# Rotary rows stored in reading order, values of four tiles kept in SBUF, and index queries loaded ahead of stores in an attention and DeltaNet layer

## The chip, the cores and the metric

The kernel runs on one core of a Trainium2 chip. The metric is the device time of one execution in microseconds; the time before is the median of three runs. Two kernels of this size can be told from each other when they differ by more than about 0.2%.

## The reference

One transformer-like layer over 2048 tokens with a model width of 1024, all in float32. In short:

```python
h = rms_norm(x, norm_mix_g)
qa, ka, va, qi, ki, wi, qb, kb, vb, zb, bb, ab = split(h @ w_in)
qa, ka, qi, ki = rope(qa), rope(ka), rope(qi), rope(ki)      # heads of 64
score[t, s] = sum_h wi[t, h] * relu(qi[t, h] . ki[s])        # 8 index heads
sel = top_k(score where s < limit(t), 256)                   # keys of each query
o_a = softmax(qa . ka[sel] / 8) @ va[sel]                    # 8 heads, 2 key heads
o_b = gated_deltanet(qb, kb, vb, zb, bb, ab)                 # 4 heads of 128
x = x + concat(o_a, o_b) @ w_out
x = x + square(relu(rms_norm(x, norm_ffn_g) @ w_ff1)) @ w_ff2
return rms_norm(x, norm_final_g)
```

Rotary embedding (rope) pairs feature i of a head with feature i + 32: each half of a head is multiplied by a cosine and added to the other half multiplied by a sine.

## The kernel before

Everything is kept transposed, features on partitions and tokens along the free dimension. The 2048 tokens are 16 tiles of 128. Three stages run one after the other, each a block in which every engine has its own queue of instructions, executed strictly in order; engines meet only at semaphores.

**Stage 1** (`norm_and_projection`) normalises x and projects the columns that the DeltaNet and the index need, into the DRAM tensor `projT`, one chunk of 128 features at a time.

**Stage 2** (`deltanet_and_selection`) runs the DeltaNet over the 16 tiles as 18 rounds of 22 slots (`ROUND`, L313). Into the same slots two planners put other work. `ProjectionPlan` (L329) puts the rest of the projection, 36 chains of 512 tokens by 128 features: index queries, attention queries (chunks 5 to 8), attention keys (chunk 9), values (chunk 10). A chain is two halves on TensorE, an eviction on ScalarE into the buffer `p_out` (`project_out`, L1104, waits until the store before it has landed) and a store by SyncE (SP) two slots later (`project_store`, L686). `SelectionPlan` (L379) puts the index scores and the search for the 256th largest score: `rotation` (L470) puts the load of a tile's index queries on SP (six transfers by `rotated_rows`, L492, and two of the rotary table), and from four slots later four steps on GpSimd (POOL), the multiply by cosine, the multiply by sine, the sum and the low part. Scores of that tile are put after the last of these, and the vector engine's share is spread over the slots by estimated costs. A load waits for the low part of the tile before, since `rot` is one buffer. In a slot, SP does the parts of the selection in the order in which they were put, and then those of the projection.

**Stage 3** (`attention_and_mlp`) overlaps attention with the output projection and the MLP. `OverlapPlan` (L1327) puts every step into numbered slots; within a slot the order of each engine is the list `ORDER` (L1335). Attention works in units, 4 for each tile (two heads each): scores against the keys, mask and exponential, transposes of the probabilities, their split into a high and a low part (`m_phi`, `m_plo`), and a product with the values. The first 16 units (tiles 0 to 3) run three slots apart, alone, before the dense matmuls begin at slot 0; this stretch is called the prelude below. From there on the dense matmuls fill TensorE and the units run beside them.

Each tile has three items to prepare (`prep_items`, L1374): its keys and two groups of four query heads. An item is loaded by SP (`prep_in`, L1639: six transfers, three for each half of the partitions), multiplied by cosine on DVE (`by_cosine`, L2012) and by sine on POOL (`by_sine`, L1738), added on POOL (`add`), rounded on ScalarE, and its low part taken on POOL (queries) or DVE (keys). Items 0 to 11 take turns in five buffers (four are rows of `m_acc`, the fifth is `m_rot`); from item 12 on all use `m_rot`, so that each load waits for the item before. The rotary table has one buffer, loaded by `table_load` (L1647), which waits until all three items of the tile before have been multiplied.

The values of a tile are loaded (`values_in`), transposed on TensorE, split into a high and a low part in the one buffer `v_split` (L1562), stored to the DRAM tensor `valsT` (`values_out`, L1659) and loaded again for each product, in pieces of at most two tiles (`values_back`, L1663), into four buffers `vals`. The load of the newest piece waits for the store:

```python
if m >= 4:
    sp.wait_ge(pv_done, m - 3)
if end == t + 1:
    sp.wait_ge(v_kept, 16 * (t + 1))
```

Weights of the dense matmuls are loaded by `weights` (L1634), rounded on ScalarE (L1848) and their low part taken on POOL (L1727); SP issues the third load only once the first of these low parts is there. In POOL's order a slot's weight split comes before the rotary steps.

Of the kernel before, what the change touches and what calls it, by code (L numbers as in the profile page):

```python
# [17 lines left out]
ALU = mybir.AluOpType  # L18
# [360 lines left out]
class SelectionPlan:  # L379
# [121 lines left out]
def deltanet_and_selection(nc, S, topk, projT, consts, mixT, biasT, scoreT, xhT, xlT, w_proj, shared, z_stored):  # L501
# [14 lines left out]
    with ExitStack() as ctx:  # L516
# [5 lines left out]
        p_out = sb("p_out", [P, 512])  # L522
# [61 lines left out]
        p_high, p_low, p_done, p_left, p_stored = map(sem, " p_high p_low p_done p_left p_stored".split())  # L584
# [51 lines left out]
        def _(sp):  # L636
# [15 lines left out]
            def selection(t, m):  # L652
                if t == 0 and m - 1 in KEY_STAGE and KEY_STAGE[m - 1] + 1 < S // KP:
                    load_keys(KEY_STAGE[m - 1] + 1)
                for kind, j in plan.at("sp", t, m):
                    if kind == "load":
# [5 lines left out]
                        if stored_chains:  # L662
                            sp.wait_ge(p_stored, 16 * (max(stored_chains) + 1))
# [64 lines left out]
            sp.wait_ge(p_stored, 16 * len(rest.chains))  # L728
# [242 lines left out]
        def _(act):  # L971
# [132 lines left out]
            def project_out(n):  # L1104
                act.wait_ge(p_done, 2 * (n + 1))
                if n:
                    act.wait_ge(p_stored, 16 * n)
                else:
                    for u in range(2):
                        act.wait_ge(z_stored[u], 16 * ((N_PROJECTED + 1 - u) // 2))  # L1110
                nc.scalar.activation(p_out[:, :], pps[:, :], ACT.Copy).then_inc(p_left, 1)
# [215 lines left out]
class OverlapPlan:  # L1327
# [72 lines left out]
    def attention(self):  # L1400
# [23 lines left out]
        for u in range(self.UN):  # L1424
# [12 lines left out]
            for i in range(self.turns(t)):  # L1437
# [9 lines left out]
                ready = kept[t] if i == self.turns(t) - 1 else self.first  # L1447
                self.put("sp", max(ready + 1, product_slot[m - 4] + 1 if m >= 4 else self.first), "values_back", u, i)
# [100 lines left out]
def attention_and_mlp(nc, S, topk, projT, consts, biasT, scoreT, valsT, mixT, xT, w_units, g_ffn, g_final, outT):  # L1549
# [5 lines left out]
    with ExitStack() as ctx:  # L1555
# [6 lines left out]
        v_split = sb("m_vsplit", [P, KV_HEADS, 2 * HD], f32r)  # L1562
# [60 lines left out]

        def prep_rows(i, half):
            r = acc[:, 2 * prep_slot(i):2 * prep_slot(i) + 2, :] if prep_slot(i) < 4 else rot[:, :, :]
            return r[:, half, 0:heads_of(i) * P].rearrange("p (h s) -> p h s", s=P)

        last_turn = lambda u: plan.turn[u, plan.turns(u // 4) - 1]
# [4 lines left out]
        def _(sp):  # L1633
# [25 lines left out]
            def values_out(t):  # L1659
                sp.wait_ge(v_done, t + 1)  # L1660
                sp.dma_start(valsT[t], v_split[:, :, :].rearrange("p g d -> p (g d)").bitcast(fp32)).then_inc(v_kept, 16)

            def values_back(u, i):  # L1663
                m, g, t = plan.turn[u, i], u % 4 // 2, u // 4
                end = min(2 * i + 2, t + 1)
                if m >= 4:
                    sp.wait_ge(pv_done, m - 3)
                if end == t + 1:
                    sp.wait_ge(v_kept, 16 * (t + 1))
                sp.dma_start(vals[:, m % 4, 0:end - 2 * i, :].bitcast(fp32),  # L1670
                             valsT[2 * i:end, :, g * P:(g + 1) * P].rearrange("c p d -> p c d")).then_inc(v_back[m % 4], 16)
# [48 lines left out]
        def _(pool):  # L1720
# [17 lines left out]
            def by_sine(i):  # L1738
                t = plan.prep_items[i][0]
                pool.wait_ge(rot_in[prep_slot(i)], 96 * (prep_turn(i) + 1))  # L1740
# [34 lines left out]
        def _(act):  # L1775
# [74 lines left out]
            def values_hi(t):  # L1850
                r = plan.ring_at["values", t]
                act.wait_ge(ring_done, r + 1)
                if t:
                    act.wait_ge(v_kept, 16 * t)
                nc.scalar.activation(v_split[:, :, 0:HD], t_bank(r)[:, 0:P].rearrange("p (g d) -> p g d", d=HD),
# [41 lines left out]
        def _(dve):  # L1897
# [95 lines left out]
            def values_low(t):  # L1993
                r = plan.ring_at["values", t]
                dve.wait_ge(v_high, t + 1)
                nc.vector.tensor_tensor(v_split[:, :, HD:2 * HD], t_bank(r)[:, 0:P].rearrange("p (g d) -> p g d", d=HD),
# [293 lines left out]
```

## Time and profile before

| | us |
|---|---|
| median of three runs | 3779.7 (3775.54 to 3780.05) |
| the profiled execution | 3773.35 |
| its span | 3771.5 |
| TensorE busy | 3343.0 (89% of the span) |
| ScalarE busy | 2162.8 (57%) |
| VectorE (DVE) busy | 2114.7 (56%) |
| GpSimd (POOL) busy | 1376.8 (37%) |

Stage 1 ends at about 489 us, stage 2 at about 1461 us and the prelude of stage 3 at about 1608 us of the span. A timeline row gives the start, the duration, the engine and line, the operation with output and inputs, and in brackets the idle time of the engine before it with what ended it. SPq rows are transfers issued by SyncE: the duration is that of the issue.

### The profile page before, as it was taken

To read this page: it belongs to the slowest core of one execution; us is meant where nothing else is said; L and a number is where in the kernel's file an instruction comes from. 1 tells how busy PE (TensorE), PEld (TensorE's weight loads), DVE (VectorE), ACT (ScalarE), POOL (GpSimd) and SP (SyncE) were. 2 spreads that over 40 slices of the span, in tenths; PEclk is the share of its full clock that TensorE was granted. 3 is DMA by queue.
4 is the path that set the end of the run, shared out by engine and by line. 5 is a ranking of instruction groups with operands and counts; after the bars stand their busy time and mean duration, and the time that the engine had idled before them with its cause. 6 is when DMAs were issued, how large, how long until landed. Compare 5 with 4: busy or idle time off the path is not lost.

```text
span 3771.5 us, 47140 instructions
## 1 busy us (share of the span) xinstructions
PE 3343.0 (89%) x16770; PEld 2754.8 (73%) x16770; DVE 2114.7 (56%) x3680; ACT 2162.8 (57%) x3717; POOL 1376.8 (37%) x721
## 2 busy tenths in 40 slices
PE   7899967888889994589999889999889999989998
PEld 5678846777777783467777768788767878867886
DVE  4223127788787762656456585757576575543223
ACT  4222127676756552477977869696877944433232
POOL 3111134435254532334444334343333333334443
PEclk8999989999999997689999999999999999999999
DMA  3521152423233333423333343333343333342232
GB/s 116 201 79 73 67 143 50 122 68 81 78 104 89 85 120 101 121 81 116 103 108 116 104 138 102 122 105 120 103 128 119 103 105 102 98 131 89 97 99 78
DMA packets 306536, 392.82 MB, mean 104 GB/s; under 512 B 24688, under 2 KB 231664, under 8 KB 301680
## 3 DMA queue, kind: packets, MB, share of 16 engines
q1 hardware_dynamic: 301552, 358.35, 31.7%
q10 hardware_dynamic: 4752, 31.46, 2.1%
q8 instruction: 135, 2.21, 0.2%
q14 instruction: 97, 0.79, 0.1%
HBM read 323.23 MB, written 66.49 MB: 103 GB/s over the span
## 4 chain that ended last, share of the span: by engine, by line
PE 27%; ACT 15%; DVE 9%; issue 5%; POOL 2%; DMA 2%; SPq 1%; ACTq 0%; DVEq 0%; POOLq 0%
PE m_ps L2083 7%; PE m_ps L2085 7%; PE m_ps L2084 7%; ACT m_junk L1784 6%; ACT m_wh L1848 2%; POOL m_wl L1727 2%; PE m_ps L2180 2%; PE m_ps L2168 2%; ACT m_prob L1875 1%; ACT m_verdict L1786 1%; ACT m_trial L1790 1%; ACT m_phi L1864 1%; PE m_ps L2153 1%; PE m_ps L2154 1%; DVE m_rl L1923 1%
## 5 line engine op out<-in xcount | busy, mean ns | idle before, releaser
L1727 POOL TENSOR_TENSOR m_wl<-m_raw,m_wh 128x1024 fp32r<-128x1024 f32 x288 | 719.4, 2498 | 1335.0 <-ACT m_wh L1848 1335.0
L2083 PE MATMUL m_ps<-m_ah,m_wh 128*128 128x512 f32 x1280 | 522.6, 408 | 24.5 <-DVE m_al L1940 17.4
L2085 PE MATMUL m_ps<-m_ah,m_wl 128*128 128x512 f32 x1280 | 507.2, 396 | 0.0
L2084 PE MATMUL m_ps<-m_al,m_wh 128*128 128x512 f32 x1280 | 505.5, 395 | 0.0
L2083 PE MATMUL m_ps<-m_th,m_wh 128*128 128x512 f32 x1024 | 415.6, 406 | 17.0 <-DVE m_tl L1925 10.1
L2085 PE MATMUL m_ps<-m_th,m_wl 128*128 128x512 f32 x1024 | 404.9, 395 | 0.0
L2084 PE MATMUL m_ps<-m_tl,m_wh 128*128 128x512 f32 x1024 | 404.4, 395 | 0.0
L1784 ACT ACTIVATE m_junk<-m_sc,m_trial 128x1152 int8<-128x1152 f32 (+7 forms) x248 | 401.5, 1619 | 2.2 <-DVE m_sc L2043 1.1
L1848 ACT ACTIVATE m_wh<-m_raw 128x1024 fp32r<-128x1024 f32 x288 | 302.8, 1051 | 153.3 <-PE m_ps L2085 137.7
L1177 DVE SCALAR_TENSOR_TENSOR i_score<-i_relu,i_w,i_score 128x512 f32<-128x512 f32 (+3 forms) x266 | 277.6, 1052 | 51.7 <-ACT i_relu L1035 38.3
L1923 DVE TENSOR_TENSOR m_rl<-m_rl 128x512 f32<-128x512 f32 x128 | 104.5, 816 | 359.3 <-ACT m_th L1804 358.9
L2083 PEld LDWEIGHTS m_ps<-m_ah,m_wh 128*128 128x128 f32 x1280 | 244.4, 191 | 79.3 <-DVE m_al L1940 20.1
L1864 ACT ACTIVATE m_phi<-m_ps 128x512 fp32r<-128x512 f32 (+1 forms) x288 | 164.2, 571 | 234.2 <-PE m_ps L2168 229.6
L2003 DVE TENSOR_TENSOR m_plo<-m_ps,m_phi 128x512 fp32r<-128x512 f32 (+1 forms) x288 | 189.2, 658 | 173.4 <-ACT m_phi L1864 171.9
L1918 DVE TENSOR_TENSOR m_acc<-m_acc,m_ps 128x512 f32<-128x512 f32 x256 | 174.8, 684 | 195.9 <-PE m_ps L2085 194.1
L2085 PEld LDWEIGHTS m_ps<-m_ah,m_wl 128*128 128x128 f32 x1280 | 243.8, 190 | 53.8
L2084 PEld LDWEIGHTS m_ps<-m_al,m_wh 128*128 128x128 f32 x1280 | 244.5, 191 | 44.1 <-issue 0.2
L2083 PEld LDWEIGHTS m_ps<-m_th,m_wh 128*128 128x128 f32 x1024 | 195.7, 191 | 57.6 <-DVE m_tl L1925 11.8
L1035 ACT ACTIVATE i_relu<-i_ps 128x512 f32<-128x512 f32 (+3 forms) x304 | 156.3, 546 | 139.8 <-PE i_ps L833 99.2
L2085 PEld LDWEIGHTS m_ps<-m_th,m_wl 128*128 128x128 f32 x1024 | 195.0, 190 | 42.8
L1983 DVE CUSTOM_DVE_ANT_0 m_prob<-m_ps,m_bias 128x512 f32<-128x512 f32 (+3 forms) x320 | 192.1, 605 | 56.8 <-PE m_ps L2154 55.0
L2084 PEld LDWEIGHTS m_ps<-m_tl,m_wh 128*128 128x128 f32 x1024 | 195.9, 191 | 36.3
(317 smaller groups left out, 7481.5 us busy)
## 6 DMA issues: line engine op xcount, KB each, us to landing
m_raw<-w_units SPq DMA_DIRECT2D x288, 512.0 KB, 3.5
m_vals<-valsT SPq DMA_DIRECT2D x256, 128.0 KB, 3.5
p_raw<-w_proj SPq DMA_DIRECT2D x72, 256.0 KB, 4.4
projT<-work ACTq DMA_DIRECT2D x12, 1024.0 KB, 3.8
g_qkvz<-projT SPq DMA_DIRECT2D x16, 768.0 KB, 6.0
wraw<-w_proj SPq DMA_DIRECT2D x21, 512.0 KB, 3.7
projT<-p_out SPq DMA_DIRECT2D x36, 256.0 KB, 3.0
work<-xT SPq DMA_DIRECT2D x8, 1024.0 KB, 5.9
```

The lines of the kernel that those rows point to most:

```text
L1035: nc.scalar.activation(relu[:, c % RELUS, 0:w], ips[:, c % 2, 0:w], ACT.Relu).then_inc(relu_done, 1)
L1177: nc.vector.scalar_tensor_tensor(out=to, in0=relu[:, c % RELUS, 0:w], scalar=w_idx[:, j, h:h + 1], in1=to, op0=ALU.mult, op1=ALU.add).then ...
L1727: nc.gpsimd.tensor_tensor(wl[:, n % 3, :], raw[:, n % 2, :], wh[:, n % 3, :].bitcast(fp32), ALU.subtract).then_inc(w_lo, 1)
L1784: turns.do(nc.scalar.activation(junk[:, 0:N], sc[:, 0:N], ACT.Sign, scale=-1.0, bias=trial[:, :].bitcast(fp32), accum_out=balance[:, :]))
L1848: nc.scalar.activation(wh[:, n % 3, :], raw[:, n % 2, :], ACT.Copy).then_inc(w_hi, 1)
L1864: nc.scalar.activation(p_hi[:, m % 2, 0:w], t_bank(r)[:, 0:w], ACT.Copy).then_inc(hi_done, 1)
L1918: nc.vector.tensor_tensor(acc[:, k, :], acc[:, k, :], f_bank("W2", b, g, k), ALU.add).then_inc(y_added, 1)
L1983: nc.vector.tensor_tensor_reduce(out=prob[:, u % 2, h, 512 * p:512 * p + w], in0=s_bank(n)[:, 0:w], in1=bias[:, 512 * p:512 * p + w], scal ...
L2003: nc.vector.tensor_tensor(p_lo[:, m % 2, 0:w], t_bank(r)[:, 0:w], p_hi[:, m % 2, 0:w].bitcast(fp32), ALU.subtract).then_inc(lo_done, 1)
L2083: nc.tensor.matmul(dst, hi, rh, start=first, stop=False)
L2084: nc.tensor.matmul(dst, hi, r_low, start=False, stop=False)
L2085: return nc.tensor.matmul(dst, lo, rh, start=False, stop=last)
```

## The change

Queries and keys of attention are stored twice, in the order in which stage 3 reads them, in two new DRAM tensors: for each feature of a head and each tile, first the heads' own rows and then the rows of the other half of the head. The store of such a chain (20 of 36) becomes six transfers. `p_out` gets two buffers with a semaphore each. In stage 3 an item is loaded by two transfers of 64 rows, contiguous in each row, and its two halves lie one behind the other in the buffer. `v_split` gets five buffers; products of tiles 0 to 3 read it directly, without the way through DRAM, and `values_back` stays for tiles 4 to 15 only. In stage 2 the load of index queries is put at the head of its slot on SP, and the POOL steps follow it by six slots instead of four.

```diff
     def rotation(self, j, slot):
         slot = max(slot, self.queries_at(j) + 1)
-        self.put("sp", slot, ("load", j))
-        slot += 4
+        self.parts.setdefault(("sp", slot), []).insert(0, ("load", j))
+        slot += 6
...
             def project_store(n):
                 b, c = rest.chains[n]
                 sp.wait_ge(p_left, n + 1)
-                sp.dma_start(projT[c, :, 512 * b:512 * (b + 1)], p_out[:, :]).then_inc(p_stored, 16)
+                if not rotated(n):
+                    sp.dma_start(projT[c, :, 512 * b:512 * (b + 1)], p_out[:, n % 2, :]).then_inc(p_stored[n % 2], 16)
+                    return
+                for h in range(2):
+                    own = p_out[HD * h:HD * (h + 1), n % 2, :].rearrange("p (t s) -> p t s", s=P)
+                    to = rowsK if c == C_KA else rowsQ[(c - C_QA) // 2]
+                    at = (h if c == C_KA else 2 * ((c - C_QA) % 2) + h) * P
+                    own_to = lambda half: to[:, 4 * b:4 * (b + 1), half, at:at + P]
+                    half = HD // 2
+                    sp.dma_start(own_to(0), own).then_inc(p_stored[n % 2], 16)
+                    sp.dma_start(own_to(1)[0:half], own[half:HD]).then_inc(p_stored[n % 2], 16)
+                    sp.dma_start(own_to(1)[half:HD], own[0:half]).then_inc(p_stored[n % 2], 16)
...
             def project_out(n):
                 act.wait_ge(p_done, 2 * (n + 1))
-                if n:
-                    act.wait_ge(p_stored, 16 * n)
-                else:
+                if n >= 2:
+                    act.wait_ge(p_stored[n % 2], stores(n % 2, n - 2))
+                elif n == 0:
...
-                ready = kept[t] if i == self.turns(t) - 1 else self.first
-                self.put("sp", max(ready + 1, product_slot[m - 4] + 1 if m >= 4 else self.first), "values_back", u, i)
+                ready = kept[t] if i == self.turns(t) - 1 else kept[t - 1] if t else self.first
+                if t >= 4:
+                    self.put("sp", max(ready + 1, product_slot[m - 4] + 1), "values_back", u, i)
...
-        v_split = sb("m_vsplit", [P, KV_HEADS, 2 * HD], f32r)
+        v_split = sb("m_vsplit", [P, 5, KV_HEADS, 2 * HD], f32r)
...
+        v_own = lambda t: v_split[:, min(t, 4), :, :]
+        back_at = lambda u, i: plan.turn[u, i] - plan.turn[16, 0]
...
-                row, n = (C_KA * P, KV_HEADS) if what == "k" else (C_QA * P + what * G * HD, G)
-                rotated_rows(sp, prep_rows(i, 0), prep_rows(i, 1),
-                             rows[row:row + n * HD, tokens(t)].rearrange("(h r) s -> r h s", r=HD), rot_in[prep_slot(i)])
+                src = (rowsK if what == "k" else rowsQ[what])[:, t].rearrange("r f n -> r (f n)")
+                for base in (0, HD):
+                    sp.dma_start(prep_flat(i)[base:base + HD], src).then_inc(rot_in[prep_slot(i)], 16)
...
             def values_hi(t):
                 r = plan.ring_at["values", t]
                 act.wait_ge(ring_done, r + 1)
-                if t:
+                if t > 4:
                     act.wait_ge(v_kept, 16 * t)
...
             def product(u, i):
                 t, m = u // 4, plan.turn[u, i]
                 chunks = range(2 * i, min(2 * i + 2, t + 1))
-                pe.wait_ge(v_back[m % 4], 16 * (m // 4 + 1))
+                if t < 4:
+                    pe.wait_ge(v_done, t + 1)
+                    v_of = lambda c: v_split[:, c, u % 4 // 2, :]
+                else:
+                    k = back_at(u, i)
+                    pe.wait_ge(v_back[k % 4], 16 * (k // 4 + 1))
+                    v_of = lambda c: vals[:, k % 4, c - 2 * i, :]
...
+    rowsQ = nc.dram_tensor("rowsQ", (2, HD, S // P, 2, 4 * P), fp32, kind="Internal").ap()
+    rowsK = nc.dram_tensor("rowsK", (HD, S // P, 2, KV_HEADS * P), fp32, kind="Internal").ap()
```

## Rows read from the trace of the kernel before

**Rows 1.** The page, TensorE's busy tenths in 40 slices of the span.
```profile
PE   7899967888889994589999889999889999989998
```

**Rows 2.** Busy time by stretch: length, each engine's busy us, clock, DMA share, GB/s.
```profile
1380.00:1430.00 50.00, 48.74 (x272) 40.53 (x271) 28.20 (x42) 26.45 (x52) 14.18 (x10) 1.00 0.37 111
1461.00:1608.00 147.00, 59.38 (x277) 47.97 (x278) 71.02 (x225) 54.55 (x139) 52.92 (x49) 0.63 0.42 119
1700.00:3771.00 2071.00, 1939.40 (x9300) 1594.55 (x9298) 1161.21 (x2046) 1320.51 (x2104) 791.15 (x359) 0.98 0.35 108
```

**Rows 3.** Timeline of SP's issues at the start of stage 3.
```profile
1463.88 0.58 SPq L496 DMA_DIRECT2D m_acc<-projT  x1
1464.50 0.59 SPq L497 DMA_DIRECT2D m_acc<-projT  x1
1465.13 0.43 SPq L498 DMA_DIRECT2D m_acc<-projT  x1
...
1481.72 10.21 SPq L1637 DMA_DIRECT2D m_raw<-w_units  x4
```

**Rows 4.** Timeline, from the first weights in to the first scores.
```profile
1485.80 1.06 ACT L1848 ACTIVATE m_wh<-m_raw 128x1024 fp32r<-128x1024 f32 x1 [14.80 <-DMA m_raw<-w_units]
1486.93 4.64 POOL L1727 TENSOR_TENSOR m_wl<-m_raw,m_wh 128x1024 fp32r<-128x1024 f32 x2 [16.38 <-ACT m_wh L1848]
...
1491.53 1.25 POOL L1742 TENSOR_TENSOR m_acc<-m_acc,m_table 128x512 f32<-128x512 f32 x1
...
1496.18 0.47 PE L2153 MATMUL m_ps<-m_keys,m_qhi 128*128 128x128 f32 x1 [26.09 <-POOL m_qlo L1755]
```

**Rows 5.** Timeline, from tile 0's last sine to tile 1's first cosine.
```profile
1496.08 1.72 POOL L1742 TENSOR_TENSOR m_acc<-m_acc,m_table 128x512 f32<-128x512 f32 x1
...
1501.42 1.94 SPq L1670 DMA_DIRECT2D m_vals<-valsT  x4
...
1503.89 0.46 SPq L1652 DMA_DIRECT2D m_table<-sinT  x1
...
1506.02 0.43 DVE L2016 TENSOR_TENSOR m_acc<-m_acc,m_table 128x256 f32<-128x256 f32 x1 [7.28 <-DMA m_table<-sinT]
```

**Rows 6.** Timeline, tile 1's last sine, and the tables of tiles 2 and 3.
```profile
1515.73 1.26 POOL L1742 TENSOR_TENSOR m_acc<-m_acc,m_table 128x512 f32<-128x512 f32 x1
...
1523.02 0.42 SPq L1652 DMA_DIRECT2D m_table<-sinT  x1
...
1525.18 0.42 DVE L2016 TENSOR_TENSOR m_acc<-m_acc,m_table 128x256 f32<-128x256 f32 x1 [4.20 <-DMA m_table<-sinT]
...
1543.10 0.43 DVE L2016 TENSOR_TENSOR m_rot<-m_rot,m_table 128x256 f32<-128x256 f32 x1 [0.93 <-DMA m_table<-sinT]
```

**Rows 7.** Timeline, the end of the prelude.
```profile
1569.63 0.58 SPq L496 DMA_DIRECT2D m_rot<-projT  x1
...
1577.15 0.69 DVE L2016 TENSOR_TENSOR m_rot<-m_rot,m_table 128x512 f32<-128x512 f32 x1 [2.91 <-DMA m_rot<-projT]
...
1598.34 0.58 SPq L496 DMA_DIRECT2D m_rot<-projT  x1
...
1601.82 0.42 SPq L1703 DMA_DIRECT2D m_tmp<-mixT  x1
```

**Rows 8.** Waits in stage 2: who for whom, us in total, times, longest.
```profile
SPq L689 <- ACT p_out L1111: 347.1, 32, 31.0
...
POOL i_rot L748 <- DMA i_table<-sinT: 63.1, 8, 15.8
...
PE p_ps L963 <- POOL p_lo L801: 17.0, 6, 4.4
...
PE i_ps L832 <- POOL i_qlo L756: 7.8, 2, 4.1
PE p_ps L963 <- ACT p_out L1111: 6.9, 4, 2.9
```

**Rows 9.** Waits of SP's queue from 1610 us to the end.
```profile
SPq L1637 <- POOL m_wl L1727: 1575.9, 271, 16.2
```

More of the change, by code:

```diff
@@ L521, in deltanet_and_selection @@
         q_hi, q_lo = sb("i_qhi", [P, 2, IDX_HEADS, P], f32r), sb("i_qlo", [P, 2, IDX_HEADS, P], f32r)
-        p_out = sb("p_out", [P, 512])
+        p_out = sb("p_out", [P, 2, 512])
         ones = sb("g_ones", [P, P])
@@ L583, in deltanet_and_selection @@
         w_in = [sem(f"p_w_in{u}") for u in range(rest.RAW)]
-        p_high, p_low, p_done, p_left, p_stored = map(sem, " p_high p_low p_done p_left p_stored".split())
+        p_high, p_low, p_done, p_left = map(sem, " p_high p_low p_done p_left".split())
+        p_stored = [sem(f"p_stored{u}") for u in range(2)]
+        rotated = lambda n: C_QA <= rest.chains[n][1] <= C_KA
+        stores = lambda u, n: 16 * sum(6 if rotated(m) else 1 for m in range(u, n + 1, 2))
         dve_s, act_s, pool_s, pe_s = sem("g_dve"), sem("g_act"), sem("g_pool"), sem("g_pe")
@@ L662, in selection @@
                         if stored_chains:
-                            sp.wait_ge(p_stored, 16 * (max(stored_chains) + 1))
+                            for u in range(2):
+                                sp.wait_ge(p_stored[u], stores(u, max(stored_chains)))
                         rotated_rows(sp, rot[:, 0], rot[:, 1], rows[C_QI * P:C_QI * P + IDX_HEADS * HD, tokens(j)]
@@ L727, in _ @@
                 sp.wait_ge(kept[u], 16 * len([z for z in plan.late_piece.values() if z % 4 == u]))
-            sp.wait_ge(p_stored, 16 * len(rest.chains))
+            for u in range(2):
+                sp.wait_ge(p_stored[u], stores(u, len(rest.chains) - 1))
         @block.gpsimd
@@ L1622, in attention_and_mlp, with prep_flat @@
         heads_of = lambda i: 2 if plan.prep_items[i][1] == "k" else 4
+        def prep_flat(i):
+            r = acc[:, 2 * prep_slot(i):2 * prep_slot(i) + 2, :] if prep_slot(i) < 4 else rot[:, :, :]
+            return r.rearrange("p f n -> p (f n)")[:, 0:2 * heads_of(i) * P]
         def prep_rows(i, half):
[L1625 to L1626 removed]
+            return prep_flat(i)[:, half * heads_of(i) * P:(half + 1) * heads_of(i) * P].rearrange("p (h s) -> p h s", s=P)
+        v_own = lambda t: v_split[:, min(t, 4), :, :]
+        back_at = lambda u, i: plan.turn[u, i] - plan.turn[16, 0]
         last_turn = lambda u: plan.turn[u, plan.turns(u // 4) - 1]
@@ L1665, in values_back @@
                 end = min(2 * i + 2, t + 1)
-                if m >= 4:
+                k = back_at(u, i)
+                if k >= 4:
                     sp.wait_ge(pv_done, m - 3)
[L1668 to L1671, printed above, removed]
+                sp.wait_ge(v_kept, 16 * (t + 1 if end == t + 1 else t))
+                sp.dma_start(vals[:, k % 4, 0:end - 2 * i, :].bitcast(fp32),
+                             valsT[2 * i:end, :, g * P:(g + 1) * P].rearrange("c p d -> p c d")).then_inc(v_back[k % 4], 16)
             def score_load(n):
@@ L2179, in product @@
                         at = 2 * P * (c - 2 * i)
-                        last = nc.tensor.matmul(o, vals[:, m % 4, c - 2 * i, :], part[:, m % 2, at:at + 2 * P],
+                        last = nc.tensor.matmul(o, v_of(c), part[:, m % 2, at:at + 2 * P],
                                                 start=(c == 0 and part is p_hi), stop=(c == t and part is p_lo))
```

27 lines of the change are left out of this document (14 added, 13 removed).

## The prediction

> **What bounds the kernel now.** I read the page's slices first, then a table of stretches, then the timelines of the stretch that stood out, then the waits of stage 2. TensorE is busy nine tenths or nearly so almost everywhere; the hole is in slices 16 and 17, at 4 and 5 tenths [rows 1]. In stretches it is the prelude of stage 3: from 1461 to 1608 us TensorE works 59.4 of 147 us, and no other engine is full either (DVE, the busiest, 71.0), while from 1700 us on it works 1939 of 2071 [rows 2]. In the prelude all engines wait on one chain after another, and SP is often its head.
>
> The hole begins with SP. The items' transfers are issued one by one: three at 1463.88, 1464.50 and 1465.13 us, the next three from 1465.61, so a half item costs 1.73 us and an item 3.47 [rows 3]. Five items, 30 transfers, come before the weights, whose first issue is at 1481.72. The weights arrive for ScalarE at 1485.80, POOL splits two of them until 1491.57, and only then comes the sine of item 1, which had long landed; its low part releases the first scores at 1496.18, after 26.1 us of waiting [rows 4]. So this start is priced by the issue of transfers that nobody needs so early, standing ahead of weights that POOL insists on.
>
> Next, tile 1's rotary table. Tile 0's last sine ends at 1497.80, but the table is issued at 1503.89: SP first issues item 6, stores the values, waits for them to land, and issues four loads of them back (1501.42 to 1503.36). DVE stands 7.3 us before tile 1's cosine and, being in order, holds up the low part of the probabilities too [rows 5]. The same pattern comes once more for tile 2, where DVE stands 4.2 us, and shrinks to 0.93 for tile 3 [rows 6]. At the prelude's end DVE stands 2.91 us for item 13, issued from 1569.63, and the fourth load of mixed rows, without which the dense matmuls don't start, is issued at 1601.82 behind the six transfers of item 15 that began at 1598.34 [rows 7].
>
> **Part by part, the start.** Ten transfers replace 30. I price each at the dearest of the old ones, 0.62 from start to start: 10 x 0.62 = 6.2 instead of 5 x 3.47 = 17.4, so the weights are issued 11.2 us earlier, near 1470.6 [rows 3]. The bytes are the same, 2.05 MB of items with 0.2 MB of table and values, and are now asked for in 6.7 us, 330 GB/s. What the queues can do: the prelude moved 119 GB/s at a DMA share of 0.42, which is 283 at a full share; the dense stretch gives 108 / 0.35 = 309 [rows 2]. At 283, 2.24 MB end 7.9 us after 1463.88, the first 0.52 MB of weights 1.9 us later, and with 2.1 us from issue to use, as the small table shows (1503.89 to 1506.02), they are usable at 1475.7 [rows 5]. By issue plus the present delay of 4.1 us (1481.72 to 1485.80) it would be 1474.7 [rows 3, 4]. I take the later: 10.1 us gained. The bounds are 11.2, and nothing if 64-row transfers run at half that rate (first rival).
>
> The Trainium skill (DMA: Bandwidth & Descriptors, section Specifications) gives an HBM limit of about 358 GB/s for a core. With it, as an estimate, the bytes would be through 1.7 us sooner and the issue would set the start, 11.1 us gained; the trace's 283 to 309 are extrapolated from shares, so neither is shown directly.
>
> **Tile 1's table.** The four loads back and the wait for the values' store go; item 6 costs two issues. The table is then held by its own condition, the sine that ended at 1497.80. A table issued at once (0.9 for two issues, 2.1 to land) lets DVE start at 1500.5 instead of 1506.0 [rows 5]. 5.5 us gained; POOL's next steps, the low part of item 2 among them, follow at the same distance. Lower bound 3 (the 1.94 us of issues and a landing of about 1), upper bound the whole 7.3.
>
> **Tiles 2 and 3.** Tile 1's last sine ends at 1516.99, the table was issued at 1523.02. Between them SP had items of six, three loads back and a wait for the store. Without these it is issued about 1.5 us after the sine (the values' store, which waits for DVE, stays ahead of it) and lands before 1520.98, when DVE arrives: 4.2 gained, and 0.9 for tile 3 in the same way [rows 6]. Bounds 2.5 and 5.1 together.
>
> **The prelude's end.** Item 13 takes 1.24 us of issue instead of 3.47, and the load back right before it is gone (about 1 us): DVE's 2.91 us vanish. Item 15 likewise gives the fourth mixed load 3.47 - 1.24 = 2.2 us [rows 7]. Together 5.1, bounds 2.2 and 5.1.
>
> Prelude: 10.1 + 5.5 + 5.1 + 5.1 = 25.8 us. Removing a wait exposes the next: behind each of these stands the units' own chain of mask, exponential, transpose and product on four engines, and TensorE at half clock for longer (mean 0.63 in the prelude [rows 2]). I take off 1 us: 25.
>
> **From the dense start on**: nothing. 36 items save 2.2 us of SP each, but SP waits there 1575.9 us in all for POOL's weight split [rows 9]. Loads back for tiles 4 to 15 keep their slots, since the product four turns before sets them, not the store of the tile before. If this cover were gone, it would be a gain.
>
> **Stage 2, more work for SP.** Twenty chains store with six transfers: 3.47 instead of about 0.4 us, 20 x 3.1 = 62 us of SP's time, and the same bytes twice. SP waits 347.1 us in this stage for `p_out` alone [rows 8], and weights are put nine slots ahead; a slot is about 2.5 us (970 us over 386). I price it at nothing; uncovered, it is up to 62. The store lasts about 3.5 us plus the landing, longer than now, but `p_out` has two buffers, and TensorE's 6.9 us of waits for it [rows 8] can only shrink.
>
> **Stage 2, the index loads.** POOL stands 63.1 us, eight times, for the index queries' table, the last of the eight transfers. Few of these reach TensorE: 17.0 us for the projection's low part, which stands behind them on POOL, and 7.8 for the index queries [rows 8]. A load that no longer stands behind the store of a search result in its slot, and two slots (5 us) more until POOL needs it, cover the shorter of the stalls and half of the long ones (15.8 at most). With 6.9 for `p_out` the ceiling is 31.7 us; DVE and ScalarE are nearly as tight there, and I take a quarter, 8.
>
> Against it stands the plan: the planner's arithmetic with six instead of four puts the last score's accumulation into slot 385 instead of 381, and the projection's last eviction is in slot 385 as well. TensorE is full there (48.7 of 50 us [rows 2]). Two pieces per slot for four slots, each two matmuls of 0.23, are 3.7 us of TensorE work moved from an early gap to the full end: plus 3.7. Bounds: 0, and four slots of 2.5, plus 10. Net for stage 2: minus 4, between minus 32 and plus 10.
>
> **Sum.** 3773.35 (the profiled execution) - 25 - 4 = 3744.4. That execution lies 6.35 us below the median of 3779.7, so for the median I forecast 3751, 0.77% faster.
>
> **Rivals.**
> *The new loads are bound by bytes.* If transfers into 64 partitions get half the rate, 141 GB/s, the weights are usable at 1463.88 + 15.9 + 3.7 + 2.1 = 1485.6 and the start gains 0.2 instead of 10.1; later items gain less too. Prelude 13 to 15, total about 18: 3762. For it: nothing that issues faster moves more bytes. Against: in the prelude the DMA share is only 0.42. By the Trainium skill (the same page, section Rules for kernel authors) two transfers to disjoint partition halves serialize on the same engines and one of 128 partitions should be used; the rule as it stands speaks of no gain from the pair, not of half rate.
> *The stalls on POOL were the path of stage 2.* Then most of the 31.7 comes: 3751 - 18 = 3733. Against it, TensorE keeps on working through the longest of them.
> *SP becomes the bound of stage 2.* The six-transfer stores stand ahead of weights, DeltaNet loads and index loads. If their 62 us reached the path, the median would be 3751 + 62 = 3813, slower; it takes more than 36 of the 62 to be slower by over 0.2%, 3787. It decides from where SP's wait for `p_out` falls to nothing in the rounds with such chains; 347 us speak against.
> *The order does not bite.* SP may stand at a wait of an earlier slot when the load's turn comes, so that putting it first in its slot changes nothing: stage 2 then only has its plus 3.7, 3759.
>
> **How the numbers follow.** The forecast with the last rival's shade, 3741 to 3761: 0.62. Bound by bytes, or a new wait in the prelude, 3761 to 3772: 0.16. Stage 2 pays more, under 3741: 0.08. Nothing within 0.2% (7.6 us, about what a measurement of this kernel can tell from no change): 0.07. Slower: 0.07. Faster is the sum of the first three, 0.86. The range 3732 to 3768 leaves out the slow cases and the ends.
>
> **What would show it.** Right: ten item transfers ahead of the weights, their first issue near 1470 us less what stage 2 gave; the first scores 25 instead of 35 us after the stage's start; DVE's cosines of tiles 1 to 3 without waits over 1 us for the table; the prelude about 122 us instead of 147; POOL's wait for the index table well under 63 us; the dense stretch unchanged in length. Wrong: weights landing over 6 us after their issue (bytes), SP with waits on it from ScalarE or POOL in stage 2 (stores), a prelude over 135 us, or a stage 2 longer than 972 us.

## The result and the profile after

The kernel after takes 3747.21 us (median, 3743.66 to 3749.72), the kernel before, run on the same chip, 3779.88: the ratio is 0.9915, with a 95% interval from 0.9903 to 0.9926. The forecast was 3751, in a range of 3732 to 3768, so sign and size came out right. The profiled execution took 3748.16 us with a span of 3746.4, 25.1 less than before's. Since the profiled execution of before lay 6 us below its median and this one lies 1 above its own, the medians differ by more, 32.7 us. Three executions further below, one of "after, weights first" (10369 us) and two of "after, again" (4269 and 14659 us), ran at a granted clock of 0.32, 0.74 and 0.22 and are left out of the medians, and nothing here shows why.

Between four marks of the timeline the span splits as follows: the first issue of stage 2 (`i_relu`), the first of stage 3 (`m_ident`), the first dense matmul, the end. "After, again" is the same kernel profiled once more, in the last experiment.

| stretch, us | before | after | after, again |
|---|---|---|---|
| stage 1 | 489.2 | 488.0 | 486.1 |
| stage 2 | 972.4 | 967.4 | 963.8 |
| prelude of stage 3 | 145.8 | 125.7 | 125.4 |
| dense stretch to the end | 2164.1 | 2165.3 | 2165.6 |

The prelude gave 20.1 us of the 25.1, stage 2 gave 5.0, and the dense stretch nothing. First the page's slices of TensorE, after:

```profile
PE   7899968888889995689999889999889999989998
```

Slices 16 and 17, at 4 and 5 before [rows 1], are at 5 and 6. The stretches, in the columns of [rows 2]:

```profile
1380.00:1430.00 50.00, 47.84 (x257) 39.38 (x255) 26.55 (x39) 26.22 (x50) 16.01 (x11) 1.00 0.40 105
1455.00:1581.00 126.00, 56.74 (x274) 45.39 (x275) 69.12 (x224) 53.41 (x137) 52.73 (x49) 0.66 0.42 118
1700.00:3746.00 2046.00, 1915.97 (x9184) 1576.26 (x9183) 1149.12 (x2023) 1294.60 (x2053) 781.24 (x354) 0.97 0.35 109
```

The prelude does the same work (DVE 69.1 us against 71.0) in 126 us instead of 147: only idle time has gone. Where it went is in the timeline. Its start, to be read beside [rows 3, 4]:

```profile
1458.96 1.13 SPq L1667 DMA_DIRECT2D m_acc<-rowsK  x2
...
1460.76 2.36 SPq L1667 DMA_DIRECT2D m_acc<-rowsQ  x4
...
1463.16 1.24 SPq L1667 DMA_DIRECT2D m_acc<-rowsK  x2
1464.44 1.24 SPq L1667 DMA_DIRECT2D m_rot<-rowsQ  x2
1465.72 12.73 SPq L1659 DMA_DIRECT2D m_raw<-w_units  x4
...
1472.32 1.06 ACT L1870 ACTIVATE m_wh<-m_raw 128x1024 fp32r<-128x1024 f32 x1 [7.62 <-DMA m_raw<-w_units]
1473.45 4.65 POOL L1749 TENSOR_TENSOR m_wl<-m_raw,m_wh 128x1024 fp32r<-128x1024 f32 x2 [9.20 <-ACT m_wh L1870]
...
1478.05 1.27 POOL L1764 TENSOR_TENSOR m_acc<-m_acc,m_table 128x512 f32<-128x512 f32 x1
...
1482.71 0.47 PE L2175 MATMUL m_ps<-m_keys,m_qhi 128*128 128x128 f32 x1 [19.66 <-POOL m_qlo L1777]
```

Ten item transfers stand ahead of the weights and take 0.6 us each. The weights are issued 10.3 us after `m_ident` instead of 20.1; ScalarE has them 16.9 us after it instead of 24.2; the first scores come at 27.3 instead of 34.6. So 9.8 us were gained at the issue and 7.3 at the scores. The tables of tiles 1 and 2 and item 13, beside [rows 5 to 7]:

```profile
1484.91 0.45 SPq L1674 DMA_DIRECT2D m_table<-sinT  x1
...
1487.08 0.43 DVE L2038 TENSOR_TENSOR m_acc<-m_acc,m_table 128x256 f32<-128x256 f32 x1 [1.81 <-DMA m_table<-sinT]
...
1501.96 0.44 DVE L2038 TENSOR_TENSOR m_acc<-m_acc,m_table 128x256 f32<-128x256 f32 x1
...
1545.72 1.09 SPq L1667 DMA_DIRECT2D m_rot<-rowsQ  x2
...
1551.95 0.69 DVE L2038 TENSOR_TENSOR m_rot<-m_rot,m_table 128x512 f32<-128x512 f32 x1 [2.10 <-DMA m_rot<-rowsQ]
```

Tile 1's cosine waits 1.8 us instead of 7.3, tile 2's shows no wait instead of 4.2. Item 13 still waits 2.1 instead of 2.9. In stage 2, the waits beside [rows 8]:

```profile
POOL i_qlo L772 <- ACT i_qhi L1044: 89.2, 11, 12.3
...
POOL i_rot L764 <- DMA i_table<-sinT: 17.6, 5, 5.8
...
PE i_ps L848 <- POOL i_qlo L772: 14.6, 4, 5.6
...
PE p_ps L979 <- POOL p_lo L817: 4.1, 2, 2.8
```

and those of SP's queue for `p_out`, now in two lines of the code, 316.5 us together against 347.1:

```profile
SPq L702 <- ACT p_out L1127: 193.8, 19, 21.9
...
SPq L694 <- ACT p_out L1127: 122.7, 14, 18.8
```

POOL's wait for the table has fallen from 63.1 to 17.6 us and TensorE's wait for `p_lo`, which stands behind it on POOL, from 17.0 to 4.1. POOL now waits for ScalarE's high part of the queries instead, and TensorE's wait for the index queries has grown from 7.8 to 14.6 us. Both of TensorE's waits for POOL together are 18.7 us instead of 24.8.

### The profile page after: what moved, and what is told of

Same layout as the page of the kernel before. It is cut to its first block, busy times and chain, and to the rows that moved or that the text cites. A ratio compares the mean times of both kernels' runs of the same rounds, so it can differ in the third digit from the quotient of the medians.

```text
span 3746.4 us, 47222 instructions
## 1 busy us (share of the span) xinstructions
PE 3338.0 (89%) x16770; PEld 2756.5 (74%) x16770; DVE 2115.7 (56%) x3680; ACT 2162.7 (58%) x3717; POOL 1376.2 (37%) x721
## 4 chain that ended last, share of the span: by engine, by line
PE 28%; ACT 15%; DVE 9%; issue 5%; POOL 2%; DMA 1%; SPq 0%; ACTq 0%; DVEq 0%; POOLq 0%
PE m_ps L2105 8%; PE m_ps L2106 7%; PE m_ps L2107 7%; ACT m_junk L1806 6%; ACT m_wh L1870 2%; PE m_ps L2208 2%; PE m_ps L2190 2%; POOL m_wl L1749 2%; ACT m_prob L1897 1%; ACT m_verdict L1808 1%; ACT m_trial L1812 1%; ACT m_phi L1886 1%; PE m_ps L2175 1%; PE m_ps L2176 1%; DVE m_rl L1945 1%
## 5 line engine op out<-in xcount | busy, mean ns | idle before, releaser
L2105 PE MATMUL m_ps<-m_th,m_wh 128*128 128x512 f32 x1024 | 415.3, 406 | 16.9 <-DVE m_tl L1947 10.1
L1870 ACT ACTIVATE m_wh<-m_raw 128x1024 fp32r<-128x1024 f32 x288 | 302.8, 1051 | 147.6 <-PE m_ps L2107 139.3
L2105 PEld LDWEIGHTS m_ps<-m_ah,m_wh 128*128 128x128 f32 x1280 | 244.8, 191 | 80.1 <-DVE m_al L1962 20.2
L1193 DVE SCALAR_TENSOR_TENSOR i_score<-i_relu,i_w,i_score 128x512 f32<-128x512 f32 (+3 forms) x266 | 253.8, 961 | 49.8 <-ACT i_relu L1051 35.5
```

What stands on the lines that cost most here:

```text
L1193: nc.vector.scalar_tensor_tensor(out=to, in0=relu[:, c % RELUS, 0:w], scalar=w_idx[:, j, h:h + 1], in1=to, op0=ALU.mult, op1=ALU.add).then ...
L1870: nc.scalar.activation(wh[:, n % 3, :], raw[:, n % 2, :], ACT.Copy).then_inc(w_hi, 1)
L2105: nc.tensor.matmul(dst, hi, rh, start=first, stop=False)
```

## The experiments

The theory (A) as of the prediction: the rows' fewer issues and the values in SBUF give the prelude's gain, each its own terms; the planner's part in stage 2 is small; all transfers of stage 3's start are bound by issue, not by bytes. The rivals: B, bytes or their layout; C, that the order on SP alone does it.

**One part alone, and all but one.** `e1_rot_only` is the kernel before with the planner's part:

```diff
-        self.put("sp", slot, ("load", j))
-        slot += 4
+        self.parts.setdefault(("sp", slot), []).insert(0, ("load", j))
+        slot += 6
```

> The kernel before with the one change in stage 2's planner (index load at the head of its slot, POOL steps six slots later instead of four). Theory A, this part gives the 5 us by which stage 2 got shorter: stage 2 (from its first issue to the first issue of stage 3) near 967 us instead of 972, POOL's wait for the index table about 18 us instead of 63, total 3775, and the prelude of stage 3 as before, 146 us to the first dense matmul. Theory B, the 5 us come from the second buffer of p_out and the stage's own scatter: stage 2 stays at 972, or grows by up to 4 us, since the plan ends four slots later.

`e2_rows_only` is the kernel before with the rows in reading order, two transfers for an item, stores by six and two buffers of `p_out`:

```diff
-                rotated_rows(sp, prep_rows(i, 0), prep_rows(i, 1),
-                             rows[row:row + n * HD, tokens(t)].rearrange("(h r) s -> r h s", r=HD), rot_in[prep_slot(i)])
...
+                for base in (0, HD):
+                    sp.dma_start(prep_flat(i)[base:base + HD], src).then_inc(rot_in[prep_slot(i)], 16)
...
```

> The kernel before with the rows in reading order only (six-transfer stores, two buffers of p_out, items of stage 3 loaded by two transfers); values and planner as before. Theory A: the weights are issued 9.8 us earlier after the start of stage 3 and used 7.3 earlier; of the waits for the tables of tiles 1 to 3 a part goes, since the items cost less issue, but the four loads of values and the wait for their store stay before them: about 3 of 11 us. Prelude near 134 us to the first dense matmul, total 3767. Theory B, the stores' 62 us of SP time cost something: stage 2 longer than 972 us.

`e3_vals_only` is the kernel before with five buffers of `v_split` that the products of tiles 0 to 3 read directly:

```diff
-        v_split = sb("m_vsplit", [P, KV_HEADS, 2 * HD], f32r)
+        v_split = sb("m_vsplit", [P, 5, KV_HEADS, 2 * HD], f32r)
...
```

> The kernel before with the values of tiles 0 to 3 kept in SBUF only; rows and planner as before. The weights are still issued 20.1 us after the stage's start, and the first scores come 35 us after it. Theory A, SP's loads of values and the wait for their store hold the tables: tile 1's table comes about 4 us earlier, tile 2's 3, prelude near 138 us, total 3772. Theory B, the item transfers alone hold SP: under 2 us.

`e4_no_rot` is the kernel after without the first of these three, so with `put` and `slot += 4`.

> The changed kernel without the change in stage 2's planner. Theory A (the planner's part gives stage 2's gain): stage 2 at 972 us, total 5 us above the changed kernel, 3752. Theory B (second buffer of p_out): stage 2 at 967 to 969 and the total as the changed kernel. The prelude is 126 us in both.

The four ran on one chip, where the kernel before took 3774.95 us:

| kernel | median us | ratio, 95% | stage 2 | prelude |
|---|---|---|---|---|
| planner's part alone | 3766.62 | 0.9968 (0.9956 to 0.9979) | 962.8 | 150.9 |
| rows alone | 3766.82 | 0.9973 (0.9961 to 0.9984) | 975.1 | 133.7 |
| values alone | 3768.55 | 0.998 (0.997 to 0.9989) | 975.6 | 139.3 |
| all but the planner's part | 3758.04 | 0.9951 (0.9935 to 0.9966) | 981.6 | 124.5 |

The prelude behaves as theory A has it: the rows take 12.1 us off 145.8, the values 6.5, both 21.3. Up to tile 3's cosine the two parts add up: the rows bring it 12.2 us earlier, the values 7.2, both 19.5. Tile 1's cosine, of its 7.3 us, still stands 5.4 with the rows alone, 4.0 with the values alone and 2.0 with both, which adds up too. The small surplus of 2.7 at the end arises behind tile 3's cosine. The planner's part was the miss: expected at 5 us or at nothing, it gave 8.3 us alone by the medians (12 by the ratio). Taken from the whole it cost 11 by the medians, which are of two chips, and 14 by the ratios. Its stage 2 is 9.6 us shorter than before's. Its own prelude is 5.1 us longer than before's, with nothing in it changed and a granted clock of 0.58 over it against 0.63. TensorE's idle time there is the same within 1 us and its busy time 4.4 us longer, so that the difference isn't one of waits.

**Which half of the planner's part.** `e7_rot_front` has the load at the head of its slot, but `slot += 4`; `e8_rot_spaced` has `slot += 6`, but `put`. All else is as after. Each undoes one of the two lines of the edit above.

> The kernel after, with only one half of the planner's change in stage 2: the load of index queries stands ahead of the stores of its slot, but the rotation follows after 4 slots as before, not 6. Theory A (what counts is that the load isn't queued behind the stores' waits): stage 2 as in the kernel after (967 us, POOL's wait for i_table 18 us); 3747 us. Theory B (the two further slots are what lets the load land): POOL's wait stays at 40 to 65 us and stage 2 gets 5 to 10 us longer; 3752 to 3758 us.

> The kernel after, with only the other half: the rotation follows 6 slots behind its load, but the load stands behind the stores of its slot as before. Theory A (order ahead of the stores counts): POOL's wait for i_table stays at 40 to 65 us, stage 2 5 to 10 us longer; 3752 to 3758 us. Theory B (the spacing counts): the wait falls to about 18 us as in the kernel after, stage 2 967 us; 3747 us.

3750.34 us (ratio 0.9918, 0.9896 to 0.9941) and 3747.08 (0.9907, 0.9882 to 0.9932): the times don't tell them apart, nor either from the kernel after. With neither half the ratio was 0.9951 (0.9935 to 0.9966): the spacing alone lies just clear of that interval, the front alone just overlaps it. With the load at the front alone, stage 2 takes 968.0 us in the profile:

```profile
POOL i_rot L764 <- DMA i_table<-sinT: 45.0, 7, 15.7
POOL i_qlo L772 <- ACT i_qhi L1044: 43.9, 9, 12.4
...
PE p_ps L979 <- POOL p_lo L817: 13.5, 4, 4.0
...
PE i_ps L848 <- POOL i_qlo L772: 8.2, 2, 4.1
```

with the spacing alone 956.9:

```profile
POOL i_qlo L772 <- ACT i_qhi L1044: 69.8, 11, 12.3
...
POOL i_rot L764 <- DMA i_table<-sinT: 46.3, 11, 11.3
...
PE i_ps L848 <- POOL i_qlo L772: 13.2, 3, 5.6
...
PE p_ps L979 <- POOL p_lo L817: 3.9, 2, 2.6
```

POOL waits as long for the table in both, 45 and 46 us. What differs is what TensorE waits for: with the spacing its wait for `p_lo` is 3.9 us instead of 13.5, and its wait for the index queries 13.2 instead of 8.2, together 17.1 instead of 21.7. So both expectations were half wrong: each half leaves POOL its 45 us, and neither is clearly slower than the kernel after. The 11 us between the two stages aren't all gain either, for the dense stretch of the second profile is 5.9 us longer than that of the first (2172.7 against 2166.8).

The length of stage 2 scatters with TensorE's busy time, which is 820 to 834 us for the same matmuls, at granted clocks of 0.94 to 0.96. The idle time of TensorE in the stage (its length less the busy time) separates the kernels better:

| planner's part | stage 2, us | TensorE idle in it, us |
|---|---|---|
| neither half (before, rows, values, all but, before with late weights) | 972.4, 975.1, 975.6, 981.6, 972.3 | 147.5, 143.8, 147.5, 147.5, 146.5 |
| load at the front alone | 968.0 | 140.5 |
| spacing alone | 956.9 | 137.3 |
| both (after, again, planner's part alone, six issues, weights late, weights first) | 967.4, 963.8, 962.8, 959.4, 960.1, 964.0 | 140.8, 138.9, 139.0, 135.4, 138.9, 138.1 |

Both halves together take 8 us of idle time (146.6 to 138.5 by the means) and 12.5 us of length. The other 4.4 are busy time, and that they belong to the change isn't shown. The front alone has 6 of the 8 and the spacing alone 9, each in one profile: each half by itself does most of the work, and they replace one another more than they add. Among the kernels with neither half, those that store reading-order rows take 975.1 and 981.6 us and the others 972.3 to 975.6; with both halves 962.8 without such stores lies amid 959.4 to 967.4 with them. So the extra stores cost nothing that stands clear of the scatter.

**Issues or layout.** `e5_six_issues` is the kernel after, each item loaded by six transfers from the same rows:

```diff
-                    sp.dma_start(prep_flat(i)[base:base + HD], src).then_inc(rot_in[prep_slot(i)], 16)
+                    flat = prep_flat(i)[base:base + HD]
+                    sp.dma_start(flat[:, 0:w], src[:, 0:w]).then_inc(rot_in[prep_slot(i)], 16)
+                    sp.dma_start(flat[0:half, w:2 * w], src[0:half, w:2 * w]).then_inc(rot_in[prep_slot(i)], 16)
+                    sp.dma_start(flat[half:HD, w:2 * w], src[half:HD, w:2 * w]).then_inc(rot_in[prep_slot(i)], 16)
...
```

> The kernel after, each item's rows loaded by six transfers again instead of two: the same bytes from the same reading-order rows. Theory A (the saving of the rows is SP's issue time): two transfers took 1.1 to 1.2 us of SP and six took about 3.2, so the weights are issued some 10 us later after the start of stage 3 (20 us instead of 10.3), the first scores come at about 37 us instead of 27.3, and the prelude (125.7 us) gets 12 to 20 us longer; 3760 to 3767 us. Theory B (it is bytes and the length of their runs that the reading order saves): the order and the lengths of the transfers are little changed, so the prelude stays within 5 us; 3747 to 3752 us.

3751.49 us (ratio 0.9922, 0.9891 to 0.9953). The weights are issued 19.5 us after the start of stage 3, the first scores come at 33.6 and the prelude takes 136.9 us, 11.2 longer than after's. That is nearly all of the 12.1 that the rows give there: the saving is mostly the issue count and not the layout (A, though 0.8 us short of its range). The total rose by 4 by the medians and by 7 in the span, less than the 12 at least that A expected and inside B's range, so the total by itself would have spoken for B. Stage 2, the same code as after's, was 8 us shorter in this profile.

**Where the weights stand.** If POOL's split of weights ahead of the first sine is the chain of the start, the weights' place is a lever of its own. `e6_weights_late` is the kernel after with the first four units and their split moved behind the rotary steps of the first tiles; `e11_weights_first` has the first two ahead of the items; `e10_late_before` is `e6`'s edit in the kernel before.

```diff
-            self.put("sp", self.first + 2 if n < 2 else self.first + 3 if n < 4 else self.unit_slot[n - 4] + 1, "weights", n)
-            s = self.unit_slot[n - 2] if n >= 2 else self.first + 5
+            self.put("sp", self.first + 24 if n < 2 else self.first + 30 if n < 4 else self.unit_slot[n - 4] + 1, "weights", n)
+            s = self.unit_slot[n - 2] if n >= 2 else self.first + 28
```

> The kernel after, with the first four weight units (2.1 MB) issued behind the rows and tables of the first tiles instead of behind the first four items, and split on ACT and POOL later. Theory A (the first sine waits for POOL, which waits for the weights' bytes: POOL L1749 took 9.3 us ahead of the first sine and 7.6 us more went in the wait for them): first scores 8 to 12 us earlier (16 to 19 us after the start of the stage instead of 27.3), prelude 5 to 12 us shorter; 3735 to 3742 us. Theory B (all these bytes have to land before the prelude's end, and the queue is busy throughout, so that only the order changes): the tables of tiles 2 and 3 or the first dense work wait instead; 3745 to 3750 us.

> The kernel after, with the first two weight units (1.05 MB) issued ahead of the items' rows and the next two behind them. Theory A (POOL's split of the weights stands ahead of the first sine, so what counts is when these bytes land): ACT takes the first unit some 5 us earlier than 16.9 us after the start of stage 3, first scores at 22 to 25 us instead of 27.3; 3742 to 3746 us. Theory B (what is ahead in the queue only changes places, the rows of the first item now wait for 1.05 MB): first scores within 2 us of 27.3; 3746 to 3750 us.

> The kernel before, with only the first four weight units moved as in the kernel with the late weights. Theory A (half of what the change gains at the start of stage 3 is that the weights' bytes no longer stand ahead of the first sine on POOL, and that is to be had by order alone): the first scores 8 to 12 us earlier than 34.6 us after the start of the stage, prelude 5 to 10 us shorter than 145.8; 3765 to 3770 us. Theory B (with six transfers for each item, SP's issues bound the prelude's first 70 us whatever the order): prelude within 3 us of 145.8; 3773 to 3777 us.

| kernel | median us | ratio, 95% | first scores | prelude |
|---|---|---|---|---|
| after, weights late | 3737.86 | 0.9887 (0.9865 to 0.9909) | 15.1 | 121.9 |
| after, weights first | 3744.45 | 0.9905 (0.9870 to 0.9939) | 22.4 | 122.0 |
| before, weights late | 3775.24 | 0.9988 (0.9976 to 1.0000) | 16.8 | 142.1 |

The second does what A expected of it, and less than `e6` at the first scores, but its prelude ends up as short. With late weights the first scores come 12.2 us earlier, at the top of A's 8 to 12, but by tile 2's cosine 8.9 of them are left and by the first dense matmul 3.8, less than A's 5 at least: the splits of the weights are the same work on POOL, only later, and tile 2's cosine waits 3.0 us for its table again, as B has it. In the kernel before the same edit brings the first scores 17.7 us earlier, and SP takes most of it back at once (nearer to B, with a prelude 3.7 us shorter and the time unchanged): tile 1's table is still issued behind the items of six transfers and the values' way through DRAM. The row:

```profile
1493.47 0.43 SPq L1652 DMA_DIRECT2D m_table<-sinT  x1
...
1495.64 0.43 DVE L2016 TENSOR_TENSOR m_acc<-m_acc,m_table 128x256 f32<-128x256 f32 x1 [14.42 <-DMA m_table<-sinT]
```

DVE's 7.3 us have become 14.4. So the early weights cost the kernel before next to nothing, order alone (C) isn't what the change lives by, and the start's gain needed the cheaper items. With late weights the kernel after is the fastest but one of the study, and its four executions (3736.71 to 3738.42) lie below all seven of the kernel after (3740.85 and more), though on another chip. Of the 9 us to after's first median the prelude shows 3.8, and the rest lies in stage 2 (960.1), whose code is the same and whose idle time is that of the second profile of after.

**More distance.** `e9_late_space8` is `e6` with `slot += 8`.

> The kernel with the late weights (3737.9 us), and in stage 2 the rotation 8 slots behind its load instead of 6. Theory A (the further slots paid because PE's wait for POOL's p_lo went from 17 us to about 4 us, and nothing of it is left to win): stage 2 955 to 968 us, 3734 to 3742 us. Theory B (each further slot of distance takes more of POOL's waits, 17.6 us for i_table and 89 us for ACT's i_qhi): stage 2 under 955 us, 3728 to 3733 us. Theory C (later queries hold up the scores and what hangs on them): stage 2 over 970 us, above 3745 us.

3735.53 us (3730.42 to 3738.24; ratio 0.9882, 0.9859 to 0.9905); stage 2 takes 956.6 us, which A covers. POOL's wait for the table is down to 3.2 us, and TensorE's for `p_lo` is up to 8.0:

```profile
PE p_ps L979 <- POOL p_lo L817: 8.0, 2, 5.7
...
POOL i_rot L764 <- DMA i_table<-sinT: 3.2, 1, 3.2
```

Against `e6` the difference is within the scatter, so that no gain is shown, as A has it; this is the lowest median of the study, by an amount that isn't shown to be real. A's reason isn't borne out: TensorE's waits for POOL grew by 3.8 us to 22.7, and yet its idle time in the stage, 133.2 us, is the lowest of all.

**The kernel after once more.**

> The kernel after once more, unchanged. Its first profile has a stage 2 of 967.4 us, while two kernels with the same stage 2 have 959.4 and 960.1. Theory A (stage 2 scatters by several us from run to run, with where the clock is granted low, and its first profile was on the long side): stage 2 957 to 963 us, prelude 125 to 126 us again, 3738 to 3745 us. Theory B (something in how this kernel meets stage 2 makes it longer, and it is fixed): stage 2 966 to 968 us again, 3745 to 3749 us.

3742.58 us (3740.85 to 3744.97), ratio 0.9907 (0.9883 to 0.993), in A's range. The prelude is 125.4 us, within 0.3 of the first profile, and stage 2 963.8, between what A and B expected. That 0.3 flatters: the five profiles with this same prelude code (with "all but" and the two halves) have 123.6 to 125.7 us, and the two with late weights 121.9 and 118.6. A prelude can be read from one profile to two or three microseconds, a stage 2 to ten or more.

## Why the prediction was right, point by point

**The bound** (the prelude as the hole, SP's issues as its head) holds: six transfers for two put 11.2 us back.

**The start**, 10.1 us forecast, gave 7.3. The issue did what was forecast (9.8 against 11.2; the third constant's load took 1.7 us to issue in this profile instead of 0.4, and in the second profile the weights stand at 9.0 and the first scores at 25.9, which is 8.7 gained). What failed is the rate: 283 GB/s, extrapolated from a share of 0.42. Here is the stretch in which the engines are full with the halves of items, and beside it one with almost only weights, from `e6_weights_late`, in the columns of [rows 2]:

```profile
1463.00:1470.00 7.00, 0.05 (x1) 0.00 (x0) 1.49 (x3) 0.42 (x1) 0.82 (x2) 0.50 1.05 242
```

```profile
1481.00:1483.00 2.00, 0.85 (x4) 0.82 (x5) 1.54 (x6) 1.50 (x6) 0.00 (x0) 0.50 0.92 363
```

242 GB/s at a full share for the halves of items with the first weights behind them, 363 for weights at 0.92. The weights were 6.6 us from issue to use instead of 4.1, and 2.5 of the 9.8 us went there. The first rival, bytes, was right in kind and wrong in size: it had 141 GB/s and no gain. The Trainium skill (DMA: Bandwidth & Descriptors, section Rules for kernel authors) says of two transfers to disjoint partition halves that they serialize and that one of 128 should be used; in this trace the halves do run below the rate of 128-partition transfers, by a third, though nothing here separates the halves from the sharing of the queues. The limit of 358 GB/s that the prediction took from the same page's section Specifications was no bound of the weights, as far as stretches of 2 us can tell (363 here, and 381 in the kernel before from 1484 to 1486 us).

**Tile 1's table**, 5.5: from the first scores to its cosine it is 9.8 us before and 4.4 after, so 5.5. **Tiles 2 and 3**, 5.1: 4.3 and 1.4, together 5.7. Both terms hold, and they need both parts: neither the rows nor the values alone bring the table's wait to 2.

**The prelude's end**, 5.1, gave 1.7 and is the term that failed most. Item 13 was to save 2.9 and saved 0.6 on the way from tile 3's cosine. Its two transfers are issued in 1.1 us instead of 3.4, but they start 0.7 us later after that cosine, and from the start of the last issue to item 13's cosine 5.7 us pass, where the last of six took 4.5 (1577.15 less 1572.64). With the same code it is 5.0 to 5.7 in the other four profiles, and with six transfers 3.5 and 3.6 in `e5_six_issues` and `e3_vals_only`, so the landing of the larger transfers took back what their issue saved.

The fourth mixed load was to save 2.2, since the dense matmuls wait for it, and it saved 1.1. The wait is as predicted. ScalarE's high part of this load stands right ahead of the last units' `m_prob`, for which TensorE waits, after:

```profile
1573.63 1.09 SPq L1667 DMA_DIRECT2D m_rot<-rowsK  x2
1574.77 0.76 SPq L1725 DMA_DIRECT2D m_tmp<-mixT  x1
...
1578.78 0.63 ACT L1863 ACTIVATE m_ah<-m_tmp 128x512 fp32r<-128x512 f32 x1 [1.26 <-DMA m_tmp<-mixT]
1579.32 0.81 ACT L1897 ACTIVATE m_prob<-m_prob,m_nmx 128x640 f32<-128x640 f32 x1
...
1580.36 1.09 PE L2190 MATMUL m_ps<-m_ident,m_prob 128*128 128x128 f32 x4 [9.82 <-ACT m_prob L1897]
```

and before, beside [rows 7]:

```profile
1605.03 0.63 ACT L1841 ACTIVATE m_ah<-m_tmp 128x512 fp32r<-128x512 f32 x1 [3.27 <-DMA m_tmp<-mixT]
1605.57 0.81 ACT L1875 ACTIVATE m_prob<-m_prob,m_nmx 128x640 f32<-128x640 f32 x1
...
1606.62 1.09 PE L2168 MATMUL m_ps<-m_ident,m_prob 128*128 128x128 f32 x4 [10.89 <-ACT m_prob L1875]
```

All fourteen profiles end their prelude with this chain. Its issue gained what was forecast: from the end of the third load's issue to the start of the fourth's 1.5 us pass instead of 3.5. But from there to its use it takes 4.0 instead of 3.2. It is 3.1 to 3.7 us in the five profiles whose item 15 has six transfers, and 3.7 to 4.0 in the nine where it has two.

So one thing was missing in all three places where the prelude fell short: the issues were saved as forecast, but what stands behind cheaper issues lands later after its own, by 2.5 us at the start, 1.2 at item 13 and 0.8 at the mixed load. Terms of the prelude: 7.3 + 5.5 + 5.7 + 1.7 = 20.2, against 25 forecast.

**The dense stretch**, nothing: 1.2 us longer, with SP's waits for the weight split at

```profile
SPq L1659 <- POOL m_wl L1749: 1651.6, 277, 16.3
```

where they were 1575.9 [rows 9]: 76 us more, about the 36 times 2.2 us of the saved issues, which so went into this wait.

**The extra stores in stage 2**, nothing: holds, within the scatter. SP's waits for `p_out` fell by 30.6 us of 347, half of the 62 us that the stores were priced at, and stage 2 doesn't follow them.

**The index loads**, minus 8 plus 3.7, net minus 4. The profiled pair says minus 5.0, and that agreement is luck: over the profiles the planner's part is worth 8 us of TensorE's idle time and 12.5 of the stage's length. The mechanism was the named one, but the price was a quarter of 31.7 us, where most of TensorE's wait for `p_lo` went (12.9 of 17.0), while that for the index queries grew by 6.8. These two make 6 of the 8; the rest isn't in these rows, and the plus 3.7 at the stage's full end didn't show by itself. The second rival, at 3733, stood for 22 us here and was about as far off on the other side. The shortfall of 5 in the prelude and the surplus of 4 to 8 in stage 2 cancelled to within 4 us of the forecast, so that the total is right in part by luck. The rival that the order doesn't bite falls: beside the kernel with neither half of the planner's part, the order alone took 23 us off POOL's wait for the table (68.2 to 45.0) and 7 off TensorE's idle time in the stage. With the spacing in place it adds nothing that shows.

## What to carry to other kernels

Judge a change in a long stage by the idle time of the bound engine, not by a helper's stall and not by the stage's length: 45 us less of POOL's wait for the table were worth 8 us of TensorE's idle time, while the length of the stage scattered by 9 us among kernels with the same planner. At the end of a chain look past the row that released the bound engine: TensorE waited for `m_prob`, but ScalarE came to it late only because a load's rounding stood ahead of it. Where transfers are many and small, count the issues ahead of the first thing that anyone waits for; but once the issues are cheap, take the rate from a stretch in which the engines are full, since one extrapolated from a share of 0.4 was a sixth too high, and expect what follows to land later after its issue. And read one profiled pair with care: here two terms missed in opposite ways and the total looked exact, which only profiles of the parts showed.

## What was not expected of the hardware

An issue on SP mostly took 0.3 to 0.62 us for anything from 32 to 512 KB. About one in twenty of those listed singly in the profile of after took longer, up to 4.0 us for a load of `w_proj` at 521.43, and 1.7 us for a constant right at the start of stage 3. Items by halves of 256 KB, with weights behind them, moved 242 GB/s at full engines, weights of 512 KB 363 at a share of 0.92, the latter over 2 us only. Stage 2 scattered by 8 to 9 us between profiles with the same planner. In stretches of 24 us its granted clock starts at 0.64 to 0.69 in each profile; from about 610 us on it reads 1.00 mostly and 0.79 to 0.99 here and there, at other places in each.
